# A hybrid decoder block: transfers reordered within an attention block, and the gathers of keys issued by ScalarE

## The reference, cut to what matters

```python
u = rms_norm(h, norm_w)
hg_q, hg_f, hg_i, hg_z, at_q, at_k, at_v, at_z = split(u @ w_in)
o_hg = hgrn2_mixer(...)                       # gated linear recurrence, 4 heads
q, k = rope(at_q), rope(at_k)                 # 8 heads of 64
for window, dilation in ((128, 1), (512, 4), (2048, 16)):
    o_i, lse_i = dilated_window_attention(q, k, v, window, dilation)
mix_w = softmax(stack(lses))
o_at = sum(mix_w * outs) * silu(at_z)
h = h + concat([o_hg, o_at]) @ w_out
return rms_norm(h, final_norm_w)
```

## Time and profile before

| | us |
|---|---|
| median of 3 runs | 1521.0 |
| the three runs | 1522.06, 1521.0, 1508.52 |
| the profiled execution, its own time | 1519.24 |
| its span, first to last instruction | 1517.4 |
| PE busy in the span | 1361.8 (90%) |
| DVE, ACT, POOL busy | 772.6, 467.9, 313.1 |
| mean granted TensorE clock | 0.951 of 2.4 GHz |

### The profile page before, as it was taken

The page is one execution under the profiler, slowest core; times in us unless marked ns, Lnnn a source line. Parts: engine busy times, 40 slices in busy tenths (PEclk is TensorE's granted clock), DMA queues, the critical chain, the costliest instruction groups (busy, mean ns, idle before and its releaser), DMA issues.

```text
span 1517.4 us, 24233 instructions
## 1 busy us (share of the span) xinstructions
PE 1361.8 (90%) x8616; PEld 1183.6 (78%) x8616; DVE 772.6 (51%) x1933; ACT 467.9 (31%) x1328; POOL 313.1 (21%) x377
## 2 busy tenths in 40 slices
PE   5999989999999997998889888988998887499997
PEld 5989979988898996986667676766777676388886
DVE  5846838665874683034544445544545453423232
ACT  5611221122121121133333344434433334411121
POOL 5632332334142122000110002100111000211010
PEclk9999999999999998999889999989999899799999
DMA  6420230131022022313343344334232335424431
GB/s 194 143 70 22 78 94 18 42 95 60 29 77 84 18 88 91 94 39 81 90 107 93 79 100 112 98 78 96 77 88 70 81 88 182 144 84 154 138 127 68
DMA packets 115568, 135.39 MB, mean 89 GB/s; under 512 B 19584, under 2 KB 85376, under 8 KB 115456
## 3 DMA queue, kind: packets, MB, share of 16 engines
q1 hardware_dynamic: 114304, 129.67, 30.1%
q10 hardware_dynamic: 1152, 4.19, 0.7%
HBM read 79.18 MB, written 29.49 MB: 72 GB/s over the span
## 4 chain that ended last, share of the span: by engine, by line
PE 33%; SPq 8%; DMA 7%; DVE 5%; ACT 4%; issue 3%; ACTq 0%; POOL 0%; DVEq 0%; POOLq 0%
PE bank L580 5%; PE bank L582 5%; PE bank L581 5%; DMA qd<-turned 4%; SPq L460 4%; PE bank L713 3%; PE bank L715 3%; PE bank L714 3%; SPq L466 2%; PE bank L768 2%; PE bank L822 2%; PE bank L761 2%; PE bank L784 1%; DVE t L1245 1%; PE bank L835 1%
## 5 line engine op out<-in xcount | busy, mean ns | idle before, releaser
L580 PE MATMUL bank<-w_hi,u_hi 128*128 128x256 f32 x768 | 222.6, 290 | 9.1 <-POOL w_lo L1098 5.1
L581 PE MATMUL bank<-w_lo,u_hi 128*128 128x256 f32 x768 | 219.1, 285 | 0.0
L582 PE MATMUL bank<-w_hi,u_lo 128*128 128x256 f32 x768 | 219.1, 285 | 0.0
L1482 DVE CUSTOM_DVE_ANT_0 p_near<-bank,near_m 128x256 f32<-128x256 f32 (+1 forms) x128 | 48.3, 414 | 297.1 <-PE bank L784 213.9
L580 PEld LDWEIGHTS bank<-w_hi,u_hi 128*128 128x128 f32 x768 | 149.3, 194 | 11.6 <-POOL w_lo L1098 5.2
L1245 DVE TENSOR_TENSOR room<-room 128x256 f32<-128x256 f32 (+6 forms) x386 | 135.9, 399 | 41.4 <-POOL room L1162 37.8
L581 PEld LDWEIGHTS bank<-w_lo,u_hi 128*128 128x128 f32 x768 | 149.5, 195 | 0.2
L582 PEld LDWEIGHTS bank<-w_hi,u_lo 128*128 128x128 f32 x768 | 149.1, 194 | 0.0
L713 PE MATMUL bank<-u_hi,w_hi 128*128 128x512 f32 x256 | 115.7, 452 | 4.0 <-issue 4.0
L1188 POOL TENSOR_TENSOR o_nf<-o_nf 128x512 f32<-128x512 f32 x16 | 25.0, 1564 | 445.4 <-DVE o_nf L1245 445.4
L822 PE MATMUL bank<-pT,far_v 128*64 128x128 f32 x640 | 66.3, 301 | 53.5 <-DMA far_v<-values 49.6
(11 more groups left out here) (164 smaller groups left out, 2942.4 us busy)
## 6 DMA issues: line engine op xcount, KB each, us to landing
qd<-turned SPq DMA_DIRECT2D x64, 256.0 KB, 4.8
stage<-in_w_groups SPq DMA_DIRECT2D x44, 256.0 KB, 3.8
room<-in_x SPq DMA_DIRECT2D x16, 512.0 KB, 4.6
values_gates<-vg_tile SPq DMA_DIRECT2D x64, 128.0 KB, 1.7
room<-values_gates SPq DMA_DIRECT2D x16, 512.0 KB, 4.5
tab<-in_rope SPq DMA_DIRECT2D x16, 512.0 KB, 5.0
ks<-turned SPq DMA_DIRECT2D x64, 128.0 KB, 3.6
xr<-in_x SPq DMA_DIRECT2D x16, 512.0 KB, 4.9
```

Of the source, the lines that this page charges most:

```text
L580: nc.tensor.matmul(dst, lhs_hi(k), rhs_hi(k), start=(k == 0), stop=False)
L581: nc.tensor.matmul(dst, lhs_hi(k), rhs_lo(k), start=False, stop=False)
L582: last = nc.tensor.matmul(dst, lhs_lo(k), rhs_hi(k), start=False, stop=(k == KT_N - 1))
L1482: nc.vector.tensor_tensor_reduce(out=dst, in0=src, in1=msk, scale=1.0, scalar=3e38, op0=ALU.add, op1=ALU.min, accum_out=stt[:, j, h:h + 1] ...
```

## The change

`PARTS` goes from 4 to 8: a filler piece is three matmuls in place of six, and twice as many are given out to each place, so each tile keeps its 18 filler matmuls. Only in tile 1 of a block three of them move from ahead of `turn_near_far0` to behind it. SP's list, ScalarE's and VectorE's are put in another order, and ScalarE's queue issues the four gathers of keys (all but those of block 0).

The diff:

```diff
-PARTS = 4
+PARTS = 8
...
         fill = filler_parts()
-        AHEAD = 3
-
-        def fillers(tile, which):
-
-            at_ = AHEAD + 3 * tile + which
-            return fill[at_:at_ + 1]
+        AHEAD = 6
+
+        def fillers(tile, first, many):
+
+            at_ = AHEAD + 6 * tile + first
+            return fill[at_:at_ + many]
...
+
+        def gather_keys(queue, n):
+
+            cols = slice((n % BLOCKS) * BT, (n % BLOCKS + 1) * BT)
+            for h in range(2):
+                for z in range(2):
+                    queue.dma_start(ks[h][64 * z:64 * z + 64, cols].bitcast(F32),
+                                    turned[z][64 + 32 * h:96 + 32 * h, :, :].bitcast(F32)).then_inc(ks_landed, 16)
...
-                if i == 3:
-                    if n + 1 < AT_BLOCKS:
-                        after(s_ready, 3 * T + 3)
-                        gather_queries(n + 1, 1)
-                        if g == 3:
-                            gather_keys(n + 1)
-                    if g == 1 and v + 1 < AT_UNITS:
-                        load_unit_piece(unit_pieces(v + 1)[0])
-                        load_unit_piece(unit_pieces(v + 1)[1])
-                    after(e_done, 4 * T + 4)
-                    sp.dma_start(stat_dram[n].rearrange("(i w) -> i w", i=P),
-                                 st_far[n % 2][:, :, :].rearrange("p a b -> p (a b)")).then_inc(stat_stored, 16)
+                if i == 3 and n + 1 < AT_BLOCKS:
+                    after(s_ready, 3 * T + 3)
+                    gather_queries(n + 1, 1)
+                    if n + 2 < AT_BLOCKS:
+                        after(b_read, n + 2)
+                        load_table(n + 2)
+                if i == 3 and g == 1 and v + 1 < AT_UNITS:
+                    load_unit_piece(unit_pieces(v + 1)[0])
+                    load_unit_piece(unit_pieces(v + 1)[1])
...
-                if i == 2:
-                    if n >= 1:
-                        after(comb_done, n)
-                        store_output(n - 1)
-                    if n + 1 < AT_BLOCKS:
-                        after(qk_lo, n + 2)
-                        if n >= 1:
-                            after(s_ready, 12 * n)
-                        gather_queries(n + 1, 0)
-                        if g != 3:
-                            gather_keys(n + 1)
-                    if n + 2 < AT_BLOCKS:
-                        after(b_read, n + 2)
-                        load_table(n + 2)
-                    if g == 2 and v + 1 < AT_UNITS:
-                        load_unit_piece(unit_pieces(v + 1)[2])
-                        load_unit_piece(unit_pieces(v + 1)[3])
...
-                if T == AT_TILES - 3:
+                if i == 2:
+                    if n >= 1:
+                        after(comb_done, n)
+                        store_output(n - 1)
+                    if n + 1 < AT_BLOCKS:
+                        after(qk_lo, n + 2)
+                        if n >= 1:
+                            after(s_ready, 12 * n)
+                        gather_queries(n + 1, 0)
+                    if g == 2 and v + 1 < AT_UNITS:
+                        load_unit_piece(unit_pieces(v + 1)[2])
+                        load_unit_piece(unit_pieces(v + 1)[3])
+                if i == 3:
+                    after(e_done, 4 * T + 4)
+                    sp.dma_start(stat_dram[n].rearrange("(i w) -> i w", i=P),
+                                 st_far[n % 2][:, :, :].rearrange("p a b -> p (a b)")).then_inc(stat_stored, 16)
+                if T == AT_TILES - 2:
                     after(z_ready, AT_BLOCKS)
                     sp.dma_start(fw[:, :], final_w).then_inc(fw_landed, 16)
...
+                scores(T, itertools.chain.from_iterable(filler_matmuls(*f) for f in fillers(T, 0, 2)))
+                mixes = T % CH == 1 and T > CH
+                if mixes:
                     spread_weights(T // CH - 1)
-                    for f in fillers(T, 1):
+                    for f in fillers(T, 2, 1):
                         filler(*f)
                 if T >= 1:
                     turn_near_far0(T - 1)
-                if not (T % CH == 1 and T > CH):
-                    for f in fillers(T, 1):
-                        filler(*f)
+                for f in fillers(T, 3, 1) if mixes else fillers(T, 2, 2):
+                    filler(*f)
                 if T >= 1:
                     turn_far1(T - 1)
-                for f in fillers(T, 2):
+                for f in fillers(T, 4, 2):
                     filler(*f)
                 if T >= 1:
                     weigh(T - 1)
...
+                if T >= 1:
+                    take_near(T - 1)
+                if i == 2 and n + 1 < AT_BLOCKS:
+                    queries_keys_hi(n + 1)
+                if T < AT_TILES:
+                    exps(T, 0)
+                if i == 3 and g == 3 and n + 1 < AT_BLOCKS:
+                    act.wait_ge(s_ready, 3 * T + 3)
+                    act.wait_ge(qk_lo, n + 2)
+                    gather_keys(nc.scalar, n + 1)
+                if T >= 1:
+                    take_far1(T - 1)
                 if i == 3:
                     act.wait_ge(z_ready, n + 1)
                     if n >= 1:
                         act.wait_ge(comb_stored, 16 * n)
                     nc.scalar.activation(gate[:, :], bank[filler_bank("Z", n)][:, :], ACT.Tanh, scale=0.5).then_inc(th_done, 1)
-                if T >= 1:
-                    take_near(T - 1)
-                if T < AT_TILES:
-                    exps(T, 0)
-                if i == 2 and n + 1 < AT_BLOCKS:
-                    queries_keys_hi(n + 1)
-                if T >= 1:
-                    take_far1(T - 1)
+                if i == 0 and 1 <= n < AT_BLOCKS:
+                    exp_differences(n - 1)
                 if T < AT_TILES:
                     exps(T, 1)
                 if T >= 1:
                     take_output(T - 1)
+                if i == 2 and g != 3 and n + 1 < AT_BLOCKS:
+                    act.wait_ge(qk_lo, n + 2)
+                    gather_keys(nc.scalar, n + 1)
...
-                if i == 0 and n >= 1:
-                    exp_differences(n - 1)
+                if T == AT_TILES:
+                    exp_differences(AT_BLOCKS - 1)
...
                 if i == 1 and n >= 1:
-                    mix_weights(n - 1)
                     weigh_outputs(n - 1)
                 if i == 0 and n >= 2:
                     dve.wait_ge(stat_stored, 16 * (n - 1))
                 lows(T, 0)
+                if i == 2 and n + 1 < AT_BLOCKS:
+                    queries_keys_lo(n + 1)
                 if T >= 1:
                     take_far0(T - 1)
                 if i == 0 and n + 1 < AT_BLOCKS:
                     rope_a(n + 1)
-                if i == 2 and n + 1 < AT_BLOCKS:
-                    queries_keys_lo(n + 1)
+                if i == 0 and n >= 1:
+                    differences(n - 1)
+                lows(T, 1)
                 if i == 3:
                     dve.wait_ge(th_done, n + 1)
                     nc.vector.scalar_tensor_tensor(out=gate[:, :], in0=gate[:, :], scalar=1.0, in1=bank[filler_bank("Z", n)][:, :],
                                                    op0=ALU.add, op1=ALU.mult).then_inc(z_done, 1)
-                lows(T, 1)
+                if i == 0 and n >= 1:
+                    mix_weights(n - 1)
                 if i == 1 and n + 1 < AT_BLOCKS:
                     rope_b(n + 1)
-                if i == 0 and n >= 1:
-                    differences(n - 1)
```

More of the change, by code:

```diff
@@ L479, in _ @@
                     after(qk_lo, 1)
-                    gather_keys(0)
+                    gather_keys(sp, 0)
                     gather_queries(0, 0)
@@ L711, in filler_matmuls @@
                     wh, wl = w_hi[1][:, :, cols], w_lo[1][:, :, cols]
[L712 to L718 removed]
+                k = part
+                yield nc.tensor.matmul(bk[:, :], wh[:, k, :], u_hi[:, k, sl], start=(k == 0), stop=False)
+                yield nc.tensor.matmul(bk[:, :], wh[:, k, :], u_lo[:, k, sl], start=False, stop=False)
+                last = nc.tensor.matmul(bk[:, :], wl[:, k, :], u_hi[:, k, sl], start=False, stop=(k == KT_N - 1))
+                if k == KT_N - 1:
+                    last.then_inc({"A": a_ready, "B": b_ready, "Z": z_ready}[kind], 1)
+                yield last
             def filler(kind, n, part):
@@ L838, in _ @@
             for T in range(AT_TILES):
-                scores(T, itertools.chain.from_iterable(filler_matmuls(*f) for f in fillers(T, 0)))
-                if T % CH == 1 and T > CH:
+                scores(T, itertools.chain.from_iterable(filler_matmuls(*f) for f in fillers(T, 0, 2)))
+                mixes = T % CH == 1 and T > CH
+                if mixes:
                     spread_weights(T // CH - 1)
-                    for f in fillers(T, 1):
+                    for f in fillers(T, 2, 1):
                         filler(*f)
```

13 lines of the change are left out of this document (removed).

## The result

The changed kernel took 1494.8 us, median of four runs (1488.3 to 1497.5), beside 1518.6 for the kernel before on the same chip: a ratio of 0.985 (95% interval 0.982 to 0.988). It is faster, by 24 us where 60 were forecast; the time lies just above the range. Of all the executions in this document one was slow, 2158.5 us of early_g3sp, and the ratios leave it out.

A forecast was written before the change was run, and what follows sets the result against it. TensorE's attention waits (90.5 us, 49.6 for far values) and the clock they lower were taken as the bound; 31.9 - 1.5 + 12 + 16 + 3 - 2 = 59.4 us saved gave 1461 us, range 1430 to 1494.

The forecast's parts named there:

- the bottleneck's successor: At block ends, once far values are issued first, the second pair of queries is what comes late next.
- (a): Twelve ordinary block ends: values first, keys on ScalarE; waits of 60.7 us become 28.8, gain 31.9 us.
- (b): ScalarE held by its four key issues: covered in ordinary blocks, later keys at g = 3; loss 1.5 us.
- (d): Kernel end, tiles 60 and 63: waits of 5.4 and 8.2 us go, plus some clock; gain 16 us (10 to 19).
- S: Moment the next block's scores can run; forecast P + 10.5, or P + 11.5 with weights.
- P: Moment TensorE begins tile 3 of a block, when the values of tile 2 can be issued.
- The DMA engines are the limit: Rival: at block ends S = P + 12 to 13.5, clock gives nothing back; 1495 us, chance 0.16.
- (c): Clock after block ends: waits of 2.4 us leave it up in half the cases; gain 12 us (0 to 24).
- (e): Tile 1, filler pieces of three matmuls: short waits for `take_near` go; gain 3 us (0 to 6).
- (f): Tile 0, differences ahead of far minima: VectorE waits for far statistics, mostly covered; loss 2 us (0 to 30).
- Statistics late: Rival: slow statistics stores make VectorE's far minima some 2 us late fifteen times; 1491 us, chance 0.06.
- The slower rival: ScalarE blocked by its key issues; slower from about 3 us per issue, 1538 us at 3.5; chance 0.04.

The follow-up runs named there:

- early_g3sp: early with the three gathers of keys at g = 3 back in SP's list behind the second pair of queries: 1466.1 us, ratio 0.967.
- keys_small: The changed kernel with each key gather of blocks 4 to 15 cut to a quarter of its columns: 1466.1 us, ratio 0.967.
- early: The changed kernel with output store and rotation table both issued in tile 2 ahead of SP's wait for the values' buffer: 1461.5 us, ratio 0.963.
- keys_sp: The changed kernel with all key gathers back in SP's list and out of ScalarE's: 1504.0 us, ratio 0.993.
- keys_act: The kernel before with its order, only the key gathers moved to ScalarE's queue: 1519.4 us, ratio 1.002.
- vals_only: The kernel before with only the values' loads in tile 2 put ahead of the rest of SP's list: 1544.9 us, ratio 1.022.
- the split of early: The changed kernel with only one move of early each: table alone 1479.6 us (0.977), store alone 1474.8 us (0.974).
- again: The changed kernel run once more, unchanged, as reference on the chip of the next three runs: 1491.1 us, ratio 0.982.

## Why the prediction was wrong

The sign, the bottleneck's successor (queries) and the size of the clock's part were right. The size of the whole failed at three steps, (a), (b) and (d): they fell short by 15.6, 5.1 and 12.8 us of the 59.4.

**(a) S = P + 10.5 and P + 11.5: mis-sized.** Measured P + 11.3 and P + 14.0. The waits at the ends of the twelve blocks fell from 60.7 to 44.4 us: a gain of 16.3 where 31.9 stood. S was reckoned from issue times, on the reading that a share of 0.72 left room for a second queue. But the 0.72 held 1.2 us in which nothing moved yet, and the engines stood at 0.93 already; in the changed kernel they were full (0.99 to 1.00), and SP's issues stretched: 2.22 for 1.23, 2.60 for 0.9. Such an issue stood in the rows already: 2.14 us for the second pair in block 14. That is the rival "The DMA engines are the limit", whose P + 12 to 13.5 was too late without weights and too early with them. Its 1495 us was the time measured, but not by its reasons: it gave the end 16 us and the clock nothing, so that the number met was luck. (By its own terms its waits fall by 12 us, not 10; and the chances that its range adds up make 0.84, not 0.82.) That bytes set S is shown by keys_small and early; issue time has its part, by keys_sp.

**(b) ScalarE held, loss 1.5 us: mis-sized at g = 3.** In ordinary blocks the four issues took 2.5 to 4.8 us, about the 3.8 assumed, and TensorE waited for `take_near` once, 1.0 us. At g = 3 they took 4.5 to 5.1 us against a full engine set, and the waits there rose from 9.0 to 15.6 us: a loss of 6.6.

**(c) The clock, gain 12 us: right in size, wrong in mechanism.** 15.3 us. I had waits of some 2.4 us leave the clock up in half of the blocks. But the first 5 us of eleven of the twelve blocks still ran at 0.50 to 0.68, after short waits too (1.88 and 1.80 us at the end of block 5, then 0.50). What changed is how long it stayed low: a hand-over and its block lost 3.4 to 5.1 us by it in the eleven blocks before, and 0 to 3.4 now. So that the sum came near is luck; why the low stretches grew shorter no run here tells apart.

**(d) The end, gain 16 us: wrong.** It gave 3.2. Both waits went, and I asked only what was late in ScalarE's list. New late were the values, 3.53 and 4.60 us, behind 4.2 MB of weights and nine loads, and a copy, 2.58. I had left 1.5 us for that. Spreading the loads, in early, gave back 7 us of the same way, 5.6 of it in the waits for values, so this is shown.

**(e) Pieces of three, gain 3 us: too high.** The short waits for `take_near` in tile 1 are gone, and 5.6 us in 15 waits for VectorE's weighed outputs are in their place; 1 to 2 us are left. Only the trace says this; no run took it alone.

**(f) Statistics, loss 2 us: right.** TensorE shows no wait for it. The rival "Statistics late" did not happen. The slower rival had the right mechanism (issues block ScalarE) at the three g = 3 blocks and in keys_act, but with no issue over 2.0 us, where it needed 3.

By the traces the sum is 16.3 - 6.6 + 15.3 + 3.2 + 1 = 29, beside 30.9 of span between the two profiled executions and 24 between the medians.

A point that the prediction did not look at is that (a) is no sum of its edits. Values first alone costs 29 us, keys on ScalarE alone nothing that counts (+3 by the ratio, interval 0 to 7); the whole gains 24. It isn't that these two need each other: keys_sp has values first and all keys in SP's list, and is 12 us faster than the kernel before and 41 faster than vals_only. What else sets these two apart is the table behind the second pair of queries in place of ahead of it, the statistics behind the values, the other engines' order in tile 3, the end and the pieces. In ordinary blocks S - P is 182.8 us in vals_only and 156.9 in keys_sp, summed. That the table's place makes the most of it fits the split of early, but no run moved it alone.

## What to carry to other kernels

When a wait at a hand-over is taken away, add up every byte that is issued between the moment the buffers come free and the moment the next stage can run, and divide by the rate that full engines reached in a row of that kind of copy, a row that begins only once they move something; if that is the later end, it is the forecast. (In block 6 values, store, keys, queries, weights and table are 3.1 MB; at 250 GB/s that is an estimated 12.6 us, and S came at P + 13.0.) The first thing to do then is to send whatever isn't needed there (stores, tables) earlier, not to a second queue. A load on another engine's queue is work in that engine's list: name what it owes next. At a kernel's end, look for bulk loads that were harmless because something slower hid them.

## What the runs showed of the hardware

The time to issue one DMA isn't a constant. The two DMAs of a pair of queries took 1.23 us in the kernel before and 2.22 in block 6 of the changed kernel; two pieces of weights 0.98 or, in early, 3.09; three gathers of keys on ScalarE's queue 1.93 or 4.53. Over the long ones the DMA share was 0.96 to 1.02. But a full set doesn't make every issue long: the second pair took 1.18 us at 914.54 and a share of 0.98. What else it takes no run here shows. The Trainium skill ("DMA: Bandwidth & Descriptors", "Issuing engines are not separate DMA queues") says that several issuers share the same 16 engines and that a second one saves only the sequencer's time. The runs agree: the second queue was worth 13 us of the kernel's 1491 (keys_sp against again), leaving out three quarters of the keys' bytes 25.

Near-full engines moved 192 to 268 GB/s in the hand-over, where gathers from one place on the chip to another are half of the bytes or more, and 384 to 411 where loads of weights and of the last stage prevail, by the table of stretches; the share was 0.89 to 1.05 in all. Here is the row of the end of the changed kernel, beside the one of 1280 us in the earlier trace rows:

```profile
1274.00:1282.00 8.00, 1.22 (x12) 0.84 (x12) 2.05 (x3) 2.99 (x5) 2.45 (x1) 0.74 1.05 384
```
